# First loads, S5 tables and first norm reordered at the head of a two-block kernel

## The chip, the core and the metric

The kernel runs on one core of a Trainium2 chip. The metric is the device time of one execution in microseconds (us), and lower is better. Its engines are named as in the profile: PE (TensorE matmul) and PEld (its weight loads), DVE (VectorE), ACT (ScalarE), POOL (GpSimd), and SP, which here only issues transfers. ACT and POOL can issue transfers too. A name with q (ACTq) is the queue side of an engine.

## The reference, cut to what matters

Two model blocks run one after the other on 512 tokens of width 1024. The change touches only the head of the first block: the norm, the projection `w_in`, and the preparation of the S5 mixer.

```
h = rmsnorm(x, mix_norm_w)                 # x 512x1024
proj = h @ w_in                            # u 256 | z 768 | xbc 1792 | dt 12 columns
# S5: 16 groups x 64 states
ab = exp(lr*dt) * (cos(li*dt) + i*sin(li*dt))
bu = einsum(u, bb);  h_t = ab * h_(t-1) + bu;  y = Re(einsum(h, c)) + u*d
# SSD: causal conv of 4 taps over xbc, silu; dt = softplus(dt_raw + bias); chunked scan
x = x + concat(y_s5, y_ssd) @ w_out
# then cross attention (mem_n = rmsnorm(mem)), conv-FFN; second block: HGRN2, FoX, routed experts
```

## The kernel before, in words

Activations lie feature by feature: `xt` is 128 partitions x 8 blocks x 512 tokens. Every fp32 operand of a projection is split into a rounded high part (ACT, lines 365 and 489) and the rest (DVE, lines 371 and 495). A projection block of 128 columns is then 8 steps of three matmuls of 128x512 (`pe_fm`, lines 415 to 417): high by high, low by high, high by low. Weights come in slots of 1 MB in a fixed order: `u`, three slots of `x` (called xa), `dt` (half as large), then x and z in turns. SP loads slot g into one of three raw buffers once the DVE has split slot g-3 (`sp_load`, line 357). ACT makes the high part once the matmuls of slot g-2 are done, DVE the low part, PE waits for that.

Each engine runs one instruction list in the order in which the code writes it, with semaphores between the engines. No scheduler is at work. The head of the program, in that order:

- ACT issues seven transfers: the parameters `prm`, `xt` blocks 0 to 3, `row`, `wglu`, the memory `mt`, and two small ones of the router's weights, which only the second block's routing reads. SP issues `xt` blocks 4 to 7, waits for ACT's half, then loads weights.
- S5's angles (`dve_s5_angle`, `act_s5_angle`): a few 128x8 operations, two sines, then nine powers of the rotation by squaring, again on DVE. POOL turns them into tables of cosines and sines over 256 time steps, by doubling: step p makes 2^p new columns for 8 state tiles, six operations of 128 x (8 x 2^p), with p from 0 to 7 (`pool_s5_tables`, lines 749 to 755).
- The first norm: ACT squares (line 450), PE sums them over partitions (line 474), ACT takes ln and exp, then DVE scales a block (line 502), ACT rounds it, DVE takes the rest (line 495), for 8 blocks. PE works on `u`'s first column block as the norm's blocks come, then on its second.
- `dve_s5_matrices` (lines 670 to 707) builds S5's input and output matrices; PE turns them (line 558), DVE copies them (`bt`, line 718).
- Five turns of `x` and `z` blocks follow (`IN_TURNS`). In turn 0 PE runs three x slots, the turn of the matrices, the memory norm's sum, and `dt` with its turn to token order. From turn 1 on each turn also carries a quarter of the S5 scan: PE makes `bu` (line 772), ACT copies it (line 795), and DVE rotates by the tables, scans and rotates back (lines 810 to 849, all 128x1024 but the scans). For an x block ACT empties the bank into `pad` (line 445), applies tap 0 (line 994), DVE the other three taps (line 904), ACT the silu (line 978).

Of the kernel before, what the change touches and what calls it, by code (L numbers as in the profile page):

```python
# [506 lines left out]

# [227 lines left out]

def pool_s5_tables(k):
    G, g, s = k.nc.gpsimd, k.g, k.s
    t1, t2 = k.tt[:, 0, :, :], k.tt[:, 1, :, :]  # L740
    g(G.memset(k.ec[:, :, 0:1], 1.0))
    g(G.memset(k.es[:, :, 0:1], 0.0))
    for p in range(8):
        n = 1 << p
        c, w = (k.pw[:, p, i, :].rearrange("p (j o) -> p j o", o=1).broadcast_to([P, 8, n]) for i in (0, 1))
        lc, ls, hc, hs = k.ec[:, :, 0:n], k.es[:, :, 0:n], k.ec[:, :, n:2 * n], k.es[:, :, n:2 * n]
# [2 lines left out]
        g(G.tensor_tensor(hc, lc, c, ALU.mult))
        g(G.tensor_tensor(t1[:, :, 0:n], ls, w, ALU.mult))  # L750
        g(G.tensor_tensor(hs, ls, c, ALU.mult))
        g(G.tensor_tensor(t2[:, :, 0:n], lc, w, ALU.mult))
        g.own()
        g(G.tensor_tensor(hc, hc, t1[:, :, 0:n], ALU.subtract))
        m = G.tensor_tensor(hs, hs, t2[:, :, 0:n], ALU.add)
        if p == 7:
# [188 lines left out]

def pe_dt(k):
    PE, s = k.nc.tensor, k.s
    pe_fm(k, "dt", 0, 0, k.hi, k.lo, cols=P)
# [4 lines left out]


def act_w_in(k):
    A, s = k.nc.scalar, k.s
# [1 line left out]
    for b in range(4):
        if b == 0:
            A.wait_ge(s.x0, 16)  # L960
        act_square(k, "mix", k.xt, k.sq0, b, T)
    act_s5_angle(k)
    for b in range(4, DB):
        if b == 4:
            A.wait_ge(s.x1, 16)
# [14 lines left out]
    for q, turn in enumerate(IN_TURNS):  # L980
        for x, (part, n) in enumerate(turn):
            stage, slot = in_slot(part, n)
            act_split_to(k, SLOT0[stage] + slot + 1)
            for j in range(2):
# [12 lines left out]
                        silu(blk - 1)  # L997
                else:
                    if n == 0 and j == 0:
                        A.wait_ge(s.s5_tab, 1)  # L1000
                    act_empty(k, i, k.sz[:, 2 * n + j, :], ACT.Silu)
            if part == "x" and n == 6:
                silu(XBC_B - 1)
# [5 lines left out]
                    act_square(k, "mem", k.mt, k.msq, b, MEM)  # L1009
        if q == 0:  # L1010
            act_split_to(k, SLOT0["dt"] + 1)
            act_norm_root(k, "mem", k.rm, k.bank[7][:, 0:MEM], D)
            act_empty(k, BLOCK0["dt"], k.gg[:, 0, 0, :])
            act_ssd_steps(k)


def dve_w_in(k):
    V, s, v = k.nc.vector, k.s, k.v
    dve_s5_angle(k)
    V.memset(k.pad[:, :, 0:3], 0.0).then_inc(s.pads_zero, 1)  # L1020
    dve_split_to(k, 0)
    dve_norm_split(k, "mix", k.xt, k.col("mix_norm", 0, DB), k.sq0, k.rs, k.hi, k.lo, 0, DB, T)
    dve_split_to(k, 1)
    dve_s5_matrices(k)
    for q, turn in enumerate(IN_TURNS):
        step = dve_s5_step(k, q - 1) if q > 0 else iter(())
        for n_, (part, n) in enumerate(turn):
            stage, slot = in_slot(part, n)
            dve_split_to(k, SLOT0[stage] + slot + 1)
            if part == "x":  # L1030
                for j in range(2):
                    blk = 2 * n + j
# [2177 lines left out]
def act_program(k):  # L3210
    A, s, ins = k.nc.scalar, k.s, k.ins
    A.dma_start(k.prm[:, :], ins["params"][0:P * NCOLS].rearrange("(p c) -> p c", p=P)).then_inc(s.params, 16)
    A.dma_start(k.xt[:, 0:4, :], ins["x_t"].rearrange("(k p) c -> p k c", p=P)[:, 0:4, :]).then_inc(s.x0, 16)
    A.dma_start(k.row[:, :], ins["rows"][0:1, :].partition_broadcast(P)).then_inc(s.rows, 16)
    A.dma_start(k.wglu[:, :, :], ins["s5_w_glu"].rearrange("(k p) c -> p k c", p=P)).then_inc(s.wglu, 16)
    A.dma_start(k.mt[:, :, :], ins["mem_t"].rearrange("(k p) c -> p k c", p=P)).then_inc(s.mem, 16)
    A.dma_start(k.wr[:, :, 0:4], ins["w_group_2"].rearrange("(k p) c -> p k c", p=P)).then_inc(s.router, 16)
    A.dma_start(k.wr[:, :, 4:20], ins["w_expert_2"].rearrange("(k p) c -> p k c", p=P)).then_inc(s.router, 16)
# [108 lines left out]
```

## Time and profile before

| what | us |
|---|---|
| median of 3 runs (lowest, highest) | 1674.35 (1672.68, 1676.23) |
| the profiled execution, its own time | 1678.19 |
| its span in the profile | 1676.9 |
| PE busy / DVE busy / ACT busy / POOL busy | 1492.6 / 1042.8 / 756.0 / 136.7 |
| mean granted TensorE clock (of full speed) | 0.939 |

The profiled execution took 1.3 us more than its span, and 3.8 us more than the median. In the page's strip of 40 slices (42 us each) PE is busy for 3 and 8 tenths in the first two slices, 4 tenths around 230 us, 6 around 1320 us and 1 in the last, and 8 or 9 tenths everywhere else. POOL is busy for 5 and 4 tenths in the first two slices and idle for most of the rest.

### The profile page before, as it was taken

What the parts mean: (1) busy time and instruction counts of PE and PEld (TensorE: products, weight loads), DVE (VectorE), ACT (ScalarE), POOL (GpSimd) and SP (SyncE); (2) the same over time, 40 slices, a digit from 0 to 9 for tenths busy, and PEclk for the clock granted to TensorE, in tenths of its full rate; (3) what the DMA queues carried; (4) which work ended last, traced back from release to release, by engine and by line L of the source; (5) the groups of instructions that cost most, each with busy time, mean ns of one, the idle gap of its engine ahead of it and who ended that gap; (6) DMA issues with size and microseconds to landing.
All of it is one profiled execution on the core that took longest, in us unless ns stands there. A gap on an engine that the chain in (4) does not pass through costs nothing.

```text
span 1676.9 us, 17418 instructions
## 1 busy us (share of the span) xinstructions
PE 1492.6 (89%) x6845; PEld 1163.3 (69%) x6845; DVE 1042.8 (62%) x1353; ACT 756.0 (45%) x994; POOL 136.7 (8%) x147
## 2 busy tenths in 40 slices
PE   3889949989988999999999999999988699999981
PEld 1666718857755788788887778786646578888861
DVE  5849976456333455445554648854443588898876
ACT  4453315564432422222223444235345568878763
POOL 5400000000000000000000022300000001111012
PEclk8898969989999999999999999999999799999996
DMA  5121204212210233232222222111002599999974
GB/s 194 63 75 51 75 26 148 74 55 75 76 50 17 106 142 114 75 113 101 101 69 69 102 100 76 51 51 51 26 1 88 215 352 413 410 410 414 407 310 176
DMA packets 41345, 231.57 MB, mean 138 GB/s; under 512 B 6448, under 2 KB 7728, under 8 KB 19120
## 3 DMA queue, kind: packets, MB, share of 16 engines
q1 hardware_dynamic: 29184, 198.75, 31.4%
q0 software_dynamic: 7584, 27.79, 4.4%
q10 hardware_dynamic: 4496, 3.91, 0.8%
q8 instruction: 55, 0.90, 0.2%
q14 instruction: 26, 0.21, 0.0%
HBM read 213.66 MB, written 16.78 MB: 137 GB/s over the span
## 4 chain that ended last, share of the span: by engine, by line
PE 75%; DVE 15%; ACT 5%; issue 3%; DMA 1%; ACTq 1%; POOL 0%; POOLq 0%; DVEq 0%
PE bank L415 14%; PE bank L416 14%; PE bank L417 14%; PE bank L2881 5%; PE bank L2883 5%; PE bank L2882 5%; PE bank L558 3%; DVE w_lo L371 2%; PE bank L434 1%; PE bank L2138 1%; PE bank L2167 1%; DVE bu L837 1%; PE bank L435 1%; PE bank L436 1%; PE bank L474 1%
## 5 line engine op out<-in xcount | busy, mean ns | idle before, releaser
L415 PE MATMUL bank<-h_hi,w_hi 128*128 128x512 f32 x952 | 393.9, 414 | 29.0 <-DVE h_lo L495 16.6
L416 PE MATMUL bank<-h_lo,w_hi 128*128 128x512 f32 x952 | 382.4, 402 | 0.0
L417 PE MATMUL bank<-h_hi,w_lo 128*128 128x512 f32 x952 | 382.0, 401 | 0.0
L371 DVE TENSOR_TENSOR w_lo<-w_raw,w_hi 128x2048 fp32r<-128x2048 f32 (+3 forms) x89 | 197.4, 2218 | 90.8 <-ACT w_hi L365 90.1
L415 PEld LDWEIGHTS bank<-h_hi,w_hi 128*128 128x128 f32 x952 | 183.8, 193 | 88.2 <-DVE h_lo L495 17.8
L417 PEld LDWEIGHTS bank<-h_hi,w_lo 128*128 128x128 f32 x952 | 183.7, 193 | 43.3
L416 PEld LDWEIGHTS bank<-h_lo,w_hi 128*128 128x128 f32 x952 | 184.3, 194 | 41.0 <-issue 1.9
L365 ACT ACTIVATE w_hi<-w_raw 128x2048 fp32r<-128x2048 f32 (+3 forms) x89 | 158.4, 1779 | 60.0 <-PE bank L417 60.0
L3061 DVE TENSOR_TENSOR h_lo<-w_raw,h_hi 128x2048 fp32r<-128x2048 f32 x32 | 73.2, 2291 | 15.4 <-ACT h_hi L2962 15.4
L3061 DVE TENSOR_TENSOR lo_b<-raw_b,hi_b 128x2048 fp32r<-128x2048 f32 x32 | 73.2, 2287 | 8.8 <-ACT hi_b L2962 8.7
L415 PE MATMUL bank<-a_hi,w_hi 128*128 128x512 f32 x176 | 69.4, 394 | 4.5 <-DVE a_lo L1579 4.5
L416 PE MATMUL bank<-a_lo,w_hi 128*128 128x512 f32 x176 | 69.7, 396 | 0.0
L417 PE MATMUL bank<-a_hi,w_lo 128*128 128x512 f32 x176 | 69.2, 393 | 0.0
L1543 ACT ACTIVATE gc<-gc 128x512 f32<-128x512 f32 x22 | 13.9, 632 | 118.6 <-DVE gc L904 118.6
L2962 ACT ACTIVATE hi_b<-raw_b 128x2048 fp32r<-128x2048 f32 x32 | 61.1, 1911 | 6.3 <-PE bank L2883 6.3
L2962 ACT ACTIVATE h_hi<-w_raw 128x2048 fp32r<-128x2048 f32 x32 | 60.9, 1908 | 0.0
L2881 PE MATMUL bank<-h_hi,hh 128*128 128x512 f32 x128 | 53.0, 414 | 5.8 <-DVE hl L3091 4.4
L2881 PE MATMUL bank<-hi_b,xh 128*128 128x512 f32 x128 | 52.9, 413 | 3.1 <-DVE xl L3068 3.1
L1577 DVE TENSOR_TENSOR gc<-gc,bank 128x512 f32<-128x512 f32 x22 | 15.1, 686 | 62.0 <-PE bank L417 62.0
L2882 PE MATMUL bank<-h_hi,hl 128*128 128x512 f32 x128 | 51.5, 403 | 0.0
L2883 PE MATMUL bank<-h_lo,hh 128*128 128x512 f32 x128 | 51.5, 403 | 0.0
L2883 PE MATMUL bank<-lo_b,xh 128*128 128x512 f32 x128 | 51.1, 399 | 0.0
(565 smaller groups left out, 2833.9 us busy)
## 6 DMA issues: line engine op xcount, KB each, us to landing
w_raw<-in_params_dram SPq DMA_DIRECT2D x122, 1024.0 KB, 4.9
raw_b<-in_params_dram SPq DMA_DIRECT2D x51, 1024.0 KB, 8.0
w_raw<-in_params_dram SPq DMA_DIRECT2D x16, 704.0 KB, 4.1
result_rows<-osb POOLq DMA_DIRECT2D x16, 512.0 KB, 8.0
result_rows<-prm POOLq DMA_DIRECT2D x8, 512.0 KB, 3.1
xt<-in_x_t_dram POOLq DMA_DIRECT2D x1, 2048.0 KB, 9.3
scratch_rows<-htm SPq DMA_DIRECT2D x4, 512.0 KB, 3.0
out_dram<-pr SPq DMA_DIRECT2D x4, 512.0 KB, 2.6
```

The costliest lines, as they stand in the source:

```text
L365: A.activation(k.w_hi[:, g % SPLIT, 0:size], k.raw[:, g % RAW, 0:size], ACT.Copy).then_inc(s.w_hi, 1)
L371: V.tensor_tensor(k.w_lo[:, g % SPLIT, 0:size], k.raw[:, g % RAW, 0:size], k.w_hi[:, g % SPLIT, 0:size].bitcast(F32), ALU.subtract).then_i ...
L415: PE.matmul(ps, wh, hi[:, c, 0:width], start=c == 0, stop=False)
L416: PE.matmul(ps, wh, lo[:, c, 0:width], start=False, stop=False)
L417: m = PE.matmul(ps, wl, hi[:, c, 0:width], start=False, stop=c == parts - 1)
L434: PE.matmul(ps, xh, wh, start=c == 0, stop=False)
L558: return k.nc.tensor.transpose(out, in_, k.ident[0:n, 0:n])
L2881: PE.matmul(o, xh[:, k0 + c, :], wh, start=first and c == 0, stop=False)
L2882: PE.matmul(o, xl[:, k0 + c, :], wh, start=False, stop=False)
L2883: m = PE.matmul(o, xh[:, k0 + c, :], wl, start=False, stop=final and c == 3)
L2962: done(A.activation(w_hi[n], raws[n], ACT.Copy), "w", n, c)
L3061: done(V.tensor_tensor(w_lo[n], raws[n], w_hi[n].bitcast(F32), ALU.subtract), "w", n, c)
```

## The change

- **Transfers.** SP's first is now `xt` 0 to 3, then weight slot 0; it waits for `xt` 4 to 7, then loads slots 1 and 2, then `mt`, `row` and `wglu`. ACT issues `prm` and `xt` 4 to 7 only. The router's two go to POOL, behind the zeroing of the result rows.
- **S5.** The two sines come behind the first norm and behind slot 1's high part on ACT; the powers (now `dve_s5_powers`) behind slot 1's low part on DVE; the matrices behind slot 3's low part in turn 0. POOL's tables wait for the powers, and stop at p = 6. DVE makes p = 7, behind the next slot's low part and ahead of the copy of `dt`.
- **PE.** 30 transposes of a constant into a bank that nothing reads come first. `u`'s two blocks take turns at each step of the norm. `dt`'s block comes ahead of the memory norm's sum, and no longer behind the wait for `bt`. Slot 0's low part on DVE lies between the norm's first and second block.

```diff
-def dve_norm_split(k, name, src, gain, sq, rs, hi, lo, off, blocks, width):
+def dve_norm_split(k, name, src, gain, sq, rs, hi, lo, off, blocks, width, slot=None):
...
             dve_norm_lo(k, name, sq, hi, lo, off, b - 1, width)
+        elif slot is not None:
+            dve_split_to(k, slot)
...
+def s5_double(k, engine, step, p):
+    n = 1 << p
...
+    step(engine.tensor_tensor(hc, lc, c, ALU.mult))
+    step(engine.tensor_tensor(t1, ls, w, ALU.mult))
+    step(engine.tensor_tensor(hs, ls, c, ALU.mult))
+    step(engine.tensor_tensor(t2, lc, w, ALU.mult))
+    step.own()
+    step(engine.tensor_tensor(hc, hc, t1, ALU.subtract))
+    return engine.tensor_tensor(hs, hs, t2, ALU.add)
...
+def dve_s5_table(k):
+    V, s = k.nc.vector, k.s
+    V.wait_ge(s.s5_tab, 1)
+    s5_double(k, V, k.v, 7).then_inc(s.s5_tab, 1)
...
 def pe_w_in(k):
+    for _ in range(30):
+        pe_turn(k, k.bank[6][:, 0:P], k.ident[:, :])
     pe_norm_sum_all(k, "mix", k.sq0, T, 7)
-    for j in range(2):
-        pe_fm(k, "u", 0, j, k.hi, k.lo, "mix")
+    for c in range(DB):
+        for j in range(2):
+            pe_fm(k, "u", 0, j, k.hi, k.lo, "mix", first=c, stop=c + 1)
...
             pe_s5_matrices(k)
+            pe_fm(k, "dt", 0, 0, k.hi, k.lo, cols=P)
             PE.wait_ge(s.s5_bt, 4)
             pe_norm_sum_all(k, "mem", k.msq, MEM, 7)
...
 def dve_w_in(k):
     dve_s5_angle(k)
-    dve_split_to(k, 0)
-    dve_norm_split(k, "mix", ..., DB, T)
+    dve_norm_split(k, "mix", ..., DB, T, slot=0)
     dve_split_to(k, 1)
-    dve_s5_matrices(k)
+    dve_s5_powers(k)
...
             dve_split_to(k, SLOT0[stage] + slot + 1)
+            if q == 0 and n_ == 1:
+                dve_s5_matrices(k)
...
             dve_split_to(k, SLOT0["dt"] + 1)
+            dve_s5_table(k)
             V.wait_ge(s.dt_turn, 1)
...
 def sp_program(k):
+    SP.dma_start(k.xt[:, 0:4, :], ...).then_inc(s.x0, 16)
+    sp_load(k, 0)
+    SP.wait_ge(s.x1, 16)
+    for g in range(1, RAW):
+        sp_load(k, g)
+    SP.dma_start(k.mt[:, :, :], ...); SP.dma_start(k.row[:, :], ...); SP.dma_start(k.wglu[:, :, :], ...)
```

ACT's list begins like this before (its seven transfers, then the S5 rate and the squares of the first four blocks of `xt`):

```order
L3212 DMA prm<-in_params_dram 128x774
L3213 DMA xt<-in_x_t_dram 128x4x512
L3214 DMA row<-in_rows_dram 128x52
L3215 DMA wglu<-in_s_w_glu_dram 128x2x256
L3216 DMA mt<-in_mem_t_dram 128x8x256
L3217 DMA w_router<-in_w_group_dram 128x8x4
L3218 DMA w_router<-in_w_expert_dram 128x8x16
L612 ACT_TABLE_LOAD
```

And like this now:

```order
L3249 DMA prm<-in_params_dram 128x774
L3250 DMA xt<-in_x_t_dram 128x4x512
L615 ACT_TABLE_LOAD
L615 ACTIVATE s5sc<-prm 128x8
L617 ACTIVATE s5sc<-s5sc 128x8
L450 ACTIVATE xbc<-xt 128x512 x8
```

Five transfers went off ACT's list, and the sines no longer part the eight squares. On DVE, the end of the angles and the start of the first norm, before:

```order
L647 TENSOR_SCALAR s5sc<-s5sc 128x8
L649 TENSOR_TENSOR s5sc<-s5sc 128x8
L651 TENSOR_SCALAR pw<-s5sc 128x8
L652 COPY pw<-s5sc 128x8
L656 TENSOR_TENSOR s5sc<-pw 128x8
L657 TENSOR_TENSOR s5sc<-pw 128x8
```

Now, at the same place (`pad`'s zeroing, then the norm's first block, slot 0's low part, the norm's second block):

```order
L650 TENSOR_SCALAR s5sc<-s5sc 128x8
L1041 MEMSET pad 128x2x3
L503 SCALAR_TENSOR_TENSOR xbc<-xt,prm,rs 128x512
L371 TENSOR_TENSOR w_lo<-w_raw,w_hi 128x2048
L503 SCALAR_TENSOR_TENSOR xbc<-xt,prm,rs 128x512
L495 TENSOR_TENSOR h_lo<-xbc,h_hi 128x512
```

The powers are gone from in front of the norm, and POOL has nothing to do until they come. On DVE at the end of turn 0, before (the last taps, the copies of S5's matrix, the next slot, the copy of `dt`):

```order
L904 SCALAR_TENSOR_TENSOR xbc<-pad,prm,xbc 128x512 x6
L718 COPY bt<-bank 128x128 x4
L371 TENSOR_TENSOR w_lo<-w_raw,w_hi 128x2048
L1044 COPY dtr<-bank 128x48
L1069 TENSOR_TENSOR sm<-dtr,row 128x48
```

Now:

```order
L727 COPY bt<-bank 128x128 x4
L371 TENSOR_TENSOR w_lo<-w_raw,w_hi 128x2048
L754 TENSOR_TENSOR ec<-ec,pw 128x8x128
L755 TENSOR_TENSOR sz<-es,pw 128x1024
L756 TENSOR_TENSOR es<-es,pw 128x8x128
L757 TENSOR_TENSOR sz<-ec,pw 128x1024
L759 TENSOR_TENSOR ec<-ec,sz 128x8x128
L760 TENSOR_TENSOR es<-es,sz 128x8x128
L1067 COPY dtr<-bank 128x48
```

The last doubling stands in DVE's list ahead of the copy of `dt`.

## Rows read from the trace of the kernel before

**Rows 1.** Chain of waits of the first 260 us: start us, us, what.

```profile
1.40 0.54 ACTq L3213
...
7.63 5.66 ACTq L3218
...
16.00 8.56 PE bank L474 x16
...
28.59 1.60 DVE xbc L502 x2
...
47.46 3.90 DVE w_lo L371
...
66.86 2.30 DVE w_lo L371
...
97.61 5.29 PE bank L474 x16
```

**Rows 2.** Transfers issued in the first 12 us: KB, median us to landing.

```profile
xt<-in_x_t_dram SPq DMA_DIRECT2D x1, 1024.0 KB, 7.4
xt<-in_x_t_dram ACTq DMA_DIRECT2D x1, 1024.0 KB, 8.9
```

**Rows 3.** Timeline of ACT: start us, us, line, operation, count [idle before <- releaser].

```profile
15.24 2.17 ACT L450 ACTIVATE xbc<-xt 128x512 f32<-128x512 f32 x4
```

**Rows 4.** Timeline of PE's weight loads in the first norm's sum.

```profile
16.99 0.34 PEld L474 LDWEIGHTS bank<-xbc,ones 128*128 128x128 f32 x1 [0.52 <-ACT xbc L450]
...
19.24 0.19 PEld L474 LDWEIGHTS bank<-xbc,ones 128*128 128x128 f32 x1 [0.24 <-issue]
```

**Rows 5.** Windows: stretch, length, busy us (count) by engine, PEclk, DMA, GB/s.

```profile
29.00:30.00 1.00, 0.00 (x0) 0.00 (x0) 1.00 (x2) 0.58 (x1) 0.92 (x2) 0.58 0.81 287
31.00:49.00 18.00, 12.99 (x25) 7.03 (x26) 18.00 (x15) 5.58 (x7) 17.61 (x14) 0.50 0.04 16
126.00:157.00 31.00, 29.61 (x113) 20.20 (x113) 28.56 (x32) 10.64 (x15) 0.00 (x0) 0.94 0.20 68
```

**Rows 6.** Timeline of DVE in a later norm, with POOL idle.

```profile
378.91 0.75 DVE L502 SCALAR_TENSOR_TENSOR xbc<-sz,prm,rs 128x512 f32<-128x512 f32 x1
379.57 0.69 DVE L495 TENSOR_TENSOR h_lo<-xbc,h_hi 128x512 fp32r<-128x512 f32 x1
```

**Rows 7.** Timeline of DVE: powers, next work, matrices, a later part of them.

```profile
19.07 0.17 DVE L649 TENSOR_TENSOR s5sc<-s5sc 128x8 f32<-128x8 f32 x1 [2.68 <-ACT s5sc L622]
...
25.07 2.40 DVE L371 TENSOR_TENSOR w_lo<-w_raw,w_hi 128x2048 fp32r<-128x2048 f32 x1
...
51.28 1.85 DVE L670 TENSOR_TENSOR s5sc<-s5sc,pw 128x8 f32<-128x8 f32 x1
...
61.62 0.16 DVE L681 TENSOR_TENSOR s5sc<-s5sc,prm 128x8 f32<-128x8 f32 x1
...
69.07 4.55 DVE L904 SCALAR_TENSOR_TENSOR xbc<-pad,prm,xbc 128x512 f32<-128x512 f32 x6
```

**Rows 8.** Timeline of ACT from the first x slot's last bank on.

```profile
65.85 0.60 ACT L445 ACTIVATE pad<-bank 128x512 f32<-128x512 f32 x1 [3.93 <-PE bank L417]
...
71.42 0.63 ACT L978 ACTIVATE xbc<-xbc 128x512 f32<-128x512 f32 x1 [2.83 <-DVE xbc L904]
...
74.42 1.90 ACT L365 ACTIVATE w_hi<-w_raw 128x2048 fp32r<-128x2048 f32 x1
76.64 0.60 ACT L445 ACTIVATE pad<-bank 128x512 f32<-128x512 f32 x1 [0.32 <-PE bank L417]
...
82.08 0.60 ACT L445 ACTIVATE pad<-bank 128x512 f32<-128x512 f32 x1 [3.46 <-PE bank L417]
```

**Rows 9.** Timeline of DVE at `dt`, of ACT at turn 1's x bank.

```profile
109.76 0.21 DVE L1044 COPY dtr<-bank 128x48 f32<-128x48 f32 x1 [10.01 <-PE bank L558]
...
120.74 0.60 ACT L445 ACTIVATE pad<-bank 128x512 f32<-128x512 f32 x1 [1.49 <-PE bank L417]
```

**Rows 10.** Groups of DVE, 126 to 250 us: count | busy us, mean ns | idle.

```profile
L810 DVE TENSOR_TENSOR gg<-bu,ec 128x1024 f32<-128x1024 f32 x4 | 4.9, 1226 | 12.4 <-ACT bu L795 12.4
```

More of the change, by code:

```diff
@@ L647, in dve_s5_angle, with dve_s5_powers @@
     V.tensor_scalar(th, th, float(np.float32(3.1415925)), float(-np.float32(3.1415925)), ALU.min, ALU.max).then_inc(s.s5_dve, 1)
+def dve_s5_powers(k):
+    V, v, s = k.nc.vector, k.v, k.s
+    mag, cs, sn, abr, abi, fr, fi, lrm, dt, th, q, r, t1, t2, den = s5_scalars(k)
     V.wait_ge(s.s5_act, 4)
@@ L733, in pe_s5_matrices @@
         pe_turn(k, k.bank[4 + n][:, 0:P], bd[:, n // 2, 4 * h:4 * h + 4, :].rearrange("p t c -> p (t c)")).then_inc(s.s5_turn, 1)
+def s5_double(k, engine, step, p):
+    n = 1 << p
+    t1, t2 = k.tt[:, 0, :, 0:n], k.tt[:, 1, :, 0:n]
+    c, w = (k.pw[:, p, i, :].rearrange("p (j o) -> p j o", o=1).broadcast_to([P, 8, n]) for i in (0, 1))
+    lc, ls, hc, hs = k.ec[:, :, 0:n], k.es[:, :, 0:n], k.ec[:, :, n:2 * n], k.es[:, :, n:2 * n]
+    step(engine.tensor_tensor(hc, lc, c, ALU.mult))
[5 more added lines that the diff above has]
+    return engine.tensor_tensor(hs, hs, t2, ALU.add)
 def pool_s5_tables(k):
     G, g, s = k.nc.gpsimd, k.g, k.s
-    t1, t2 = k.tt[:, 0, :, :], k.tt[:, 1, :, :]
     g(G.memset(k.ec[:, :, 0:1], 1.0))
     g(G.memset(k.es[:, :, 0:1], 0.0))
[L743 to L746, printed above, removed]
+    for p in range(7):
         g.own()
         G.wait_ge(s.s5_pow, p + 1)
[L749 to L756, printed above, removed]
+        m = s5_double(k, G, g, p)
+        if p == 6:
             m.then_inc(s.s5_tab, 1)
@@ L805, in dve_s5_step @@
     V.wait_ge(s.s5_buc, 4 * q + 4)
-    V.wait_ge(s.s5_tab, 1)
+    V.wait_ge(s.s5_tab, 2)
+    v.own()
     if q > 0:
@@ L947, in pe_dt @@
     PE, s = k.nc.tensor, k.s
-    pe_fm(k, "dt", 0, 0, k.hi, k.lo, cols=P)
     PE.wait_ge(s.evac_a, EMPTIED[BLOCK0["dt"]][1])
@@ L957, in act_w_in @@
     act_s5_rate(k)
[L958 to L965, printed above, removed]
+    for b in range(DB):
+        if b in (0, 4):
+            A.wait_ge(s.x1 if b else s.x0, 16)
         act_square(k, "mix", k.xt, k.sq0, b, T)
@@ L972, in act_w_in @@
     act_split_to(k, 1)
+    act_s5_angle(k)
     for j in range(2):
@@ L999, in act_w_in @@
                     if n == 0 and j == 0:
-                        A.wait_ge(s.s5_tab, 1)
+                        A.wait_ge(s.s5_tab, 2)
                     act_empty(k, i, k.sz[:, 2 * n + j, :], ACT.Silu)
@@ L1011, in act_w_in @@
             act_split_to(k, SLOT0["dt"] + 1)
+            act_empty(k, BLOCK0["dt"], k.gg[:, 0, 0, :])
             act_norm_root(k, "mem", k.rm, k.bank[7][:, 0:MEM], D)
-            act_empty(k, BLOCK0["dt"], k.gg[:, 0, 0, :])
             act_ssd_steps(k)
@@ L1020, in dve_w_in @@
     V.memset(k.pad[:, :, 0:3], 0.0).then_inc(s.pads_zero, 1)
-    dve_split_to(k, 0)
-    dve_norm_split(k, "mix", k.xt, k.col("mix_norm", 0, DB), k.sq0, k.rs, k.hi, k.lo, 0, DB, T)
+    dve_norm_split(k, "mix", k.xt, k.col("mix_norm", 0, DB), k.sq0, k.rs, k.hi, k.lo, 0, DB, T, slot=0)
     dve_split_to(k, 1)
-    dve_s5_matrices(k)
+    dve_s5_powers(k)
     for q, turn in enumerate(IN_TURNS):
@@ L2327, in pool_zero, with pool_router @@
         G.dma_start(results[n], source).then_inc(s.zeroed, 16)
+def pool_router(k):
+    G, s = k.nc.gpsimd, k.s
+    G.dma_start(k.wr[:, :, 0:4], k.ins["w_group_2"].rearrange("(k p) c -> p k c", p=P)).then_inc(s.router, 16)
+    G.dma_start(k.wr[:, :, 4:20], k.ins["w_expert_2"].rearrange("(k p) c -> p k c", p=P)).then_inc(s.router, 16)
 def pe_w_out2_turn(k, b):
@@ L3189, in sp_program @@
 def sp_program(k):
-    k.nc.sync.dma_start(k.xt[:, 4:8, :], k.ins["x_t"].rearrange("(k p) c -> p k c", p=P)[:, 4:8, :]).then_inc(k.s.x1, 16)
-    k.nc.sync.wait_ge(k.s.x0, 16)
-    for g in range(SLOTS):
+    SP, s, ins = k.nc.sync, k.s, k.ins
+    SP.dma_start(k.xt[:, 0:4, :], ins["x_t"].rearrange("(k p) c -> p k c", p=P)[:, 0:4, :]).then_inc(s.x0, 16)
+    sp_load(k, 0)
+    SP.wait_ge(s.x1, 16)
+    for g in range(1, RAW):
+        sp_load(k, g)
+    SP.dma_start(k.mt[:, :, :], ins["mem_t"].rearrange("(k p) c -> p k c", p=P)).then_inc(s.mem, 16)
+    SP.dma_start(k.row[:, :], ins["rows"][0:1, :].partition_broadcast(P)).then_inc(s.rows, 16)
+    SP.dma_start(k.wglu[:, :, :], ins["s5_w_glu"].rearrange("(k p) c -> p k c", p=P)).then_inc(s.wglu, 16)
+    for g in range(RAW, SLOTS):
         sp_load(k, g)
@@ L3202, in pool_program @@
     pool_zero(k)
+    pool_router(k)
     pool_mix(k)
@@ L3212, in act_program @@
     A.dma_start(k.prm[:, :], ins["params"][0:P * NCOLS].rearrange("(p c) -> p c", p=P)).then_inc(s.params, 16)
[L3213 to L3218, printed above, removed]
+    A.dma_start(k.xt[:, 4:8, :], ins["x_t"].rearrange("(k p) c -> p k c", p=P)[:, 4:8, :]).then_inc(s.x1, 16)
     act_w_in(k)
```

## The prediction

> **What bounds the kernel now.** I read the page's strip first: PE is busy nearly everywhere but in the first slice and around 230 us. The change works on the first 126 us, so I followed the chain of waits there [rows 1], then the timelines of single engines.
>
> The chain begins on ACT. It issues transfers until 7.63 + 5.66 = 13.3 us, the last a small router load. ACT's half of `xt`, issued at 1.40 [rows 1], landed 8.9 later, at 10.3, and SP's half, its first transfer, issued at about 0.9, landed 7.4 later, at 8.3 [rows 2]. The squares start at 15.2 [rows 3]. PE sums from 16.00 to 24.56, and DVE scales the first block at 28.59 [rows 1], so 4.03 us of ACT lie between. The norm's split takes DVE from 28.59 to 47.46, 18.9 us for 16 operations, 1.18 each [rows 1]. A later norm, with POOL idle, goes from one operation to the next in 379.57 - 378.91 = 0.66 us [rows 6]. POOL's table work lies beside the slow one, and the low part of slot 1 takes 3.90 beside it where slot 2's takes 2.30 alone [rows 1]. So the two engines take turns at something. Then DVE builds the matrices from 51.28 to 66.86 [rows 7, 1], PE stands until 69.2, finishes its third x slot at 92.9 (82.08 + 2 x 5.44 [rows 8]), waits for `bt` until 97.61, sums for 5.29, and does `dt` [rows 1]. DVE waits 10.0 us and copies `dt` at 109.76 [rows 9]. From 126 to 250 us DVE sets the pace: busy for 28.56 of 31.0 us [rows 5], and what idle time is left is mostly the 12.4 us for `bu` in four turns [rows 10].
>
> **The change, step by step, in the profiled execution's time.**
>
> *Start.* ACT issues two transfers instead of seven and is free at 2 us (1.40 + 0.54 [rows 1]). SP's first load should land as its first did, at 8.3 us. The squares start there, and PE's sum 0.76 later as before (15.24 to 16.00) [rows 1, 3], at 9.1. It took 8.56. Its weight loads show a slow phase, 0.34 each until nearly 19 us, then 0.19 [rows 4]: 3 us at half rate, of which a warm start saves 1.5. The 30 transposes would give that warm start if the clock is held over the 1 or 2 us between; after PE stopped at 24.56 the fall came within the window 29 to 30 [rows 5], which speaks for it. Bounds: end at 16.1 or 17.7; I take 16.5, nearer to the held clock. DVE scales at 16.5 + 4.0 = 20.5 instead of 28.6: 8.1 gained.
>
> The Trainium skill (DMA: Bandwidth & Descriptors, section Queues, rings and completion order) says that each DMA engine goes round-robin between the queue rows that have work. That speaks against the new order: slot 0 now follows on SP's queue and would take half the engines' time from ACT's `xt` half. No row has this mix. By that rule the half that landed at 10.3 would lose about 2 us more; PE needs its fifth block at 9.1 + 4 x 0.86 = 12.5, so the sum stays as it is, or loses under 1 us.
>
> *Split.* 16 operations at 0.66, plus slot 0's low part, 2.3 (before, it lay in the wait for the norm): 12.9, so DVE ends at 33.4. Slot 1's high part follows the last rounding, and its low part ends at about 37. PE starts `u` after the first low part, at 20.5 + 0.66 + 2.3 + 1.3 = 24.8. Two steps of `u` are 6 matmuls. A block of 24 matmuls takes 5.44 us at the full clock (82.08 - 76.64) [rows 8], 0.227 each; at half clock 6 of them need 2.6 us, more than DVE's 1.3, so PE is never idle and should leave the low clock, as it did in the norm's sum, in 3 us. `u` ends at 24.8 + 10.9 + 1.5 = 37.2, where slot 1 is ready. The first x slot ends at 37.2 + 10.9 = 48.1. Before, that was 65.8 [rows 8].
>
> *To the matrices.* On ACT the way from that slot's last bank to the end of slot 3's high part took from 65.85 to 76.32 with 2.83 of waiting for DVE's taps [rows 8]: 7.6 without. The wait should go, as DVE is ahead: powers 6.0 (25.07 - 19.07 [rows 7]) to 43, slot 2's low part to 45 to 47, taps of the first block (half of 4.55, rows 7; more beside POOL) to 50. So slot 3's high part ends at 55.7, its low part at 58.0. POOL's p = 4 to 6 fall in 44 to 58; I add 1.0 for operations that wait one POOL operation, so 59.0. The other slots on PE end at 48.1 + 2 x 10.9 = 69.9; PE is not the bound.
>
> *DVE to `dt`.* The matrices took 15.6 beside POOL; the part from 61.62 on, alone, took 5.2 [rows 7, 1]. The nine operations before it are of the 0.2 us kind, 1.7 in all: 6.9, to 65.9. Then 12 taps, 2 x 4.55 [rows 7], with `dt`'s low part, half of 2.3, between: 10.3, to 76.2. Four copies of `bt` of 0.2 and a low part: 3.1, to 79.3. The last doubling: 6 x 1.2 [rows 10] = 7.2, to 86.5. PE meanwhile does `dt` from 72 to 77, sums by 82 and turns `dt` by 83: the order that put 5.4 us of `dt` into the wait for `bt` now makes DVE the later one. Without the table DVE would wait for PE instead, so 3.5 of its 7.2 are on the path. The copy of `dt` comes at 86.5 instead of 109.76: 23.3 gained.
>
> *To S5.* Before, ACT waited 1.49 for PE at the last x bank [rows 9]; now PE has that bank at 94, ACT comes at 96, so the 1.5 is gained too. Total 24.8. I take off 0.6 for the extra wait between engines in the ping-pong of taps and silus: 24.2. The scan's turns follow unchanged, as nothing in them has an absolute time. The router's loads cost nothing on POOL: the page's strip shows it idle there, and their first reader is the second block's routing.
>
> 1678.2 - 24.2 = 1654.0 in the profiled execution. The median of the runs lies 3.8 below it, so 1650.2.
>
> **Rivals.**
>
> *A. DVE and POOL share more than I charge.* p = 0 to 6 now lie beside the powers, slot 2 and the taps of the first x slot. From 28.6 to 51.3 DVE did 10.6 + 2.3 of work in 22.8 us, so the pair cost 9.9, and the nine small operations of the matrices lost about 8.6 (51.28 to 61.62 [rows 7] less 1.7). What moved to DVE was under that last loss. If all of the first 9.9 comes back on the path, the gain is 24.2 - 9.9 + 1.0 = 15.3: 1659. For it: DVE is nearly the bound there. Against: DVE has slack until 56 us, where ACT is the later one.
>
> *B. The clock stays low through `u`.* 48 matmuls at 0.43 are 20.5 instead of 12.4: 8 lost, some in DVE's slack, gain 16 to 18: 1657. For it: from 31 to 49 us PE was at 0.50 [rows 5]. Against: it was busy for 13.0 of those 18 us, and now its work is dense.
> The Trainium skill (TensorE: Matmul & The Clock Gate, Part 1) says that the idle state is the throttled one and that activity releases it, so an idle stretch behind the 30 transposes can undo them. By that rule the sum would end at 17.7, and 1.2 us of the gain go; the trace agrees that it falls after idling, but only 4.5 us later.
>
> *C. More than I think:* DVE's and ACT's exchange of taps and silus closes up, slot 3 comes earlier, PE is the bound to 70 and DVE copies at 83: gain 28, 1646.
>
> *D. Slower: the scan's turns become PE's.* In 126 to 250 us PE has 113 matmul records a turn beside DVE's 31 us, at a clock of 0.94 in the first [rows 5]. If its clock fell in the turns, since it is ahead and waits more, it would need 113 x 0.227 = 25.7 us at full and 51 at half clock. From a quarter of its matmuls at half clock on PE decides instead of DVE; the 24 are lost when each of some 3.3 turns costs 7.3 more, that is when half of them run so, and at all of them it is slower by 3.3 x 20 - 24 = 42: 1676 to 1716. Against: before, PE idled by the same pattern and fell only to about 0.9.
>
> *E. Nothing gained:* a hidden wait, as for a load behind `mt`, holds turn 0 at its old time: 1674. Slots 1 and 2 have over 15 us to land, which speaks against it.
>
> **How the numbers follow.** Forecast 0.66, its own range 1646.5 to 1655. A 0.14, B 0.08, C 0.08, D 0.02, E 0.02. The range 1645 to 1660 holds the forecast and nearly all of A, B and C. The bound for same is 0.2%, 3.3 us, about what a measurement of this kernel can tell. Faster 0.96, same 0.02, slower 0.02.
>
> **What would show it.** Right: the first norm sum starting near 9 and DVE scaling at 20 to 22; 0.66 from one norm operation to the next; PE without a gap from 25 to 70; DVE without a gap from 59 to 87; POOL ending its tables before 60; the turns of 31 us as before. Wrong: a sum that starts after 11 (the transfers), norm operations over 0.9 (not POOL, then), a gap ahead of x slot 2 or 3 on PE, a copy of `dt` after 92, or turns longer than 32.

## The result and the profile after

The changed kernel takes 1653.2 us (median of 4 runs, 1651.9 to 1654.5), the kernel before, on the same chip, 1673.5 us. The ratio is 0.9879, 95% interval 0.9864 to 0.9894: 20.3 us faster, 3 us less than forecast, inside the range. The profiled execution took 1652.19 us (span 1651.0).

The chain of waits of the kernel after, from its first 90 us (start us, us, what), answers [rows 1]:

```profile
1.40 11.18 DMA xt<-in_x_t_dram
12.60 0.64 ACT xbc L450
13.28 3.71 PE bank L474 x8
...
21.02 0.75 DVE xbc L503
21.78 2.20 DVE w_lo L371
...
55.76 1.82 ACT w_hi L365
57.60 3.02 DVE w_lo L371
...
79.92 2.20 DVE w_lo L371
82.12 1.14 DVE ec L754
```

ACT's seven transfers no longer lead the chain: `xt` does. From 57.6 to 89 us it lies on DVE without a break. The transfers of the kernel after (issuing queue, KB, median us to landing) answer [rows 2]:

```profile
xt<-in_x_t_dram SPq DMA_DIRECT2D x1, 1024.0 KB, 7.4
xt<-in_x_t_dram ACTq DMA_DIRECT2D x1, 1024.0 KB, 11.2
```

SP's half lands as before, ACT's takes 11.2 instead of 8.9 us and lands at 12.6. The timelines of ACT and of PE (start us, us, what, [idle before <- releaser]) show the squares and the norm's sum in two parts, with that hole between them [rows 3]:

```profile
8.31 2.19 ACT L450 ACTIVATE xbc<-xt 128x512 f32<-128x512 f32 x4 [1.72 <-DMA xt<-in_x_t_dram]
12.60 2.19 ACT L450 ACTIVATE xbc<-xt 128x512 f32<-128x512 f32 x4 [2.10 <-DMA xt<-in_x_t_dram]
```

```profile
8.99 3.70 PE L474 MATMUL bank<-xbc,ones 128*128 128x512 f32 x8 [1.02 <-ACT xbc L450]
13.28 3.70 PE L474 MATMUL bank<-xbc,ones 128*128 128x512 f32 x8 [0.59 <-ACT xbc L450]
```

Both parts take 3.70 for 8 matmuls, the full clock's pace; the slow first 3 us of [rows 4] are gone. The timeline of DVE of the kernel after, in the norm, at the first small operations of the matrices, and from `bt` to the first rotation, answers [rows 7, 9]:

```profile
25.16 0.74 DVE L503 SCALAR_TENSOR_TENSOR xbc<-xt,prm,rs 128x512 f32<-128x512 f32 x1
25.82 0.68 DVE L495 TENSOR_TENSOR h_lo<-xbc,h_hi 128x512 fp32r<-128x512 f32 x1
...
57.60 3.02 DVE L371 TENSOR_TENSOR w_lo<-w_raw,w_hi 128x2048 fp32r<-128x2048 f32 x1 [3.05 <-ACT w_hi L365]
60.54 1.24 DVE L679 TENSOR_TENSOR s5sc<-s5sc,pw 128x8 f32<-128x8 f32 x1
61.70 0.15 DVE L680 TENSOR_TENSOR s5sc<-s5sc 128x8 f32<-128x8 f32 x1
61.78 1.26 DVE L681 TENSOR_TENSOR s5sc<-s5sc 128x8 f32<-128x8 f32 x1
...
79.05 0.88 DVE L727 COPY bt<-bank 128x128 f32<-128x128 f32 x4
...
88.98 0.20 DVE L1067 COPY dtr<-bank 128x48 f32<-128x48 f32 x1
...
104.09 1.23 DVE L832 TENSOR_TENSOR gg<-bu,ec 128x1024 f32<-128x1024 f32 x1 [1.94 <-ACT bu L816]
```

Norm operations follow each other at 0.66 us, as where POOL is idle [rows 6]. The low part of slot 3 takes 3.02 instead of 2.3, and two small operations last 1.25, because POOL's tables end only at 63.0 (timeline of POOL, kernel after):

```profile
58.54 3.21 POOL L759 TENSOR_TENSOR ec<-ec,sz 128x512 f32<-128x512 f32 x1
61.72 1.30 POOL L760 TENSOR_TENSOR es<-es,sz 128x512 f32<-128x512 f32 x1
```

The windows of the kernel after (stretch, length, busy us (count) of PE, PEld, DVE, ACT, POOL, then PEclk, DMA, GB/s) answer [rows 5]; the third and fourth go from one turn's first rotation to the next:

```profile
25.00:28.00 3.00, 2.61 (x6) 2.17 (x7) 3.00 (x6) 1.57 (x3) 0.00 (x0) 0.50 0.82 322
31.00:49.00 18.00, 18.00 (x81) 14.89 (x80) 15.00 (x52) 9.07 (x11) 10.76 (x30) 1.00 0.25 78
104.09:135.67 31.58, 31.35 (x114) 21.76 (x113) 28.56 (x33) 10.94 (x15) 0.00 (x0) 0.88 0.20 67
135.67:168.12 32.45, 31.80 (x114) 21.80 (x113) 28.56 (x33) 10.93 (x15) 0.00 (x0) 0.87 0.18 65
```

From 31 to 49 us PE works at 2.4 GHz without a gap (granted 1.00), where it stood for 5 of the 18 us and worked at 1.2 GHz (0.50). In the first turn DVE's busy time is the same 28.56 us, but PE is busy for nearly the whole turn at a mean clock of 0.88. That is no mark of the changed kernel: cut from rotation to rotation, the kernel before has one turn at 0.94 and one at 0.87 (windows, kernel before):

```profile
126.24:157.54 31.30, 29.91 (x114) 20.50 (x113) 28.56 (x33) 10.95 (x15) 0.00 (x0) 0.94 0.19 68
157.54:189.40 31.86, 31.49 (x114) 21.72 (x113) 28.55 (x33) 10.94 (x15) 0.00 (x0) 0.87 0.19 66
```

The group of the first rotations, 104 to 228 us after (count | busy us, mean ns | idle), answers [rows 10]; DVE waits 13.5 instead of 12.4 us there:

```profile
L832 DVE TENSOR_TENSOR gg<-bu,ec 128x1024 f32<-128x1024 f32 x4 | 4.9, 1226 | 13.5 <-ACT bu L816 13.5
```

**Where the time came from.** In the profiled executions, the copy of `dt` comes 20.8 us earlier (109.76 to 88.98), the first rotation 22.15 (126.24 to 104.09), and the first rotation of the fourth turn 21.3 (224.75 to 203.47). After that both kernels run the same code. The same norm operation is 23.0 earlier (378.91 [rows 6] to 355.94), the same low part further on 25.5 (timelines of DVE, before, then after):

```profile
621.36 2.29 DVE L371 TENSOR_TENSOR w_lo<-w_raw,w_hi 128x2048 fp32r<-128x2048 f32 x1 [1.11 <-ACT w_hi L365]
```

```profile
595.83 2.29 DVE L371 TENSOR_TENSOR w_lo<-w_raw,w_hi 128x2048 fp32r<-128x2048 f32 x1 [1.11 <-ACT w_hi L365]
```

Those last 4 us are not the change's. From the first rotation of the fourth turn to this low part the code is the same in all fourteen traces of this document, and that stretch took from 391.3 to 396.6 us in them; before it was 396.6, the longest, after it was 392.4. The profiled execution of before also lay 4.7 above its median (1678.2 to 1673.5), that of after 1.0 below its own. What the change gave by the end of the stage, 21.3, is about the 20.3 of the medians.

### The profile page after: what moved, and what is told of

Read it like the earlier page. It is cut to its first block, busy times and chain, and to the rows that moved or that the text cites. A ratio compares the mean times of both kernels' runs of the same rounds, so it can differ in the third digit from the quotient of the medians.

```text
span 1651.0 us, 17477 instructions
## 1 busy us (share of the span) xinstructions
PE 1485.6 (90%) x6875; PEld 1163.2 (70%) x6875; DVE 1034.1 (63%) x1359; ACT 756.0 (46%) x994; POOL 121.3 (7%) x143
## 4 chain that ended last, share of the span: by engine, by line
PE 75%; DVE 13%; ACT 6%; issue 4%; DMA 2%; POOL 0%; POOLq 0%; ACTq 0%; DVEq 0%
PE bank L415 14%; PE bank L416 14%; PE bank L417 14%; PE bank L2910 5%; PE bank L2912 5%; PE bank L2911 5%; PE bank L561 3%; DVE w_lo L371 2%; PE bank L434 1%; PE bank L2161 1%; PE bank L2190 1%; PE bank L435 1%; PE bank L436 1%; DVE xbc L926 1%; DVE bu L859 1%
## 5 line engine op out<-in xcount | busy, mean ns | idle before, releaser
L1566 ACT ACTIVATE gc<-gc 128x512 f32<-128x512 f32 x22 | 13.9, 632 | 118.5 <-DVE gc L926 118.5
```

## The experiments

Three marks are read in every trace, in us from its start: DVE's copy of `dt`, the first S5 rotation (called the marker in the expectations), and the first rotation of the fourth turn. The marks come from one profiled execution each. Where the ratio says "one execution", the time does too; otherwise times are medians, and each ratio is to the kernel before on the same chip (its medians lay from 1673.3 to 1674.7).

| kernel | time us | ratio [95%] | copy of `dt` | first rotation | fourth turn |
|---|---|---|---|---|---|
| before | 1673.5 | 1 | 109.76 | 126.24 | 224.75 |
| after | 1653.2 | 0.9879 [0.9864, 0.9894] | 88.98 | 104.09 | 203.47 |
| after, again | 1653.0 | 0.9868 [0.9845, 0.9891] | 88.87 | 105.28 | 203.31 |
| loads only | 1666.9 | 0.9962 [0.9948, 0.9975] | 103.17 | 119.28 | 217.72 |
| powers first | 1657.4 | 0.9905 [0.9888, 0.9922] | 92.74 | 109.16 | 207.38 |
| last table on POOL | 1663.8 | 0.9944 [0.9923, 0.9964] | 97.03 | 113.16 | 212.22 |
| no transposes | 1656.0 | one execution | 90.72 | 106.78 | 203.41 |
| sum first | 1654.2 | one execution | 92.73 | 109.05 | 206.58 |
| slot 0 later | 1651.4 | one execution | 88.79 | 104.48 | 203.32 |
| `u` in a row | 1655.0 | one execution | 89.37 | 105.79 | 202.44 |
| split early | 1648.9 | 0.9853 [0.9836, 0.9870] | 86.68 | 103.05 | 199.80 |
| early, squares late | 1652.0 | 0.9863 [0.9846, 0.9879] | 89.29 | 105.70 | 203.71 |
| squares late | 1656.7 | 0.9888 [0.9862, 0.9914] | 91.01 | 107.14 | 203.80 |
| early, matrices late | 1651.3 | 0.9872 [0.9855, 0.9889] | 86.71 | 101.84 | 201.23 |

**1. Loads only.** The kernel before, with the new `sp_program`, `act_program` and `pool_router` and nothing else.

> The kernel before with the new order of loads alone (SP, ACT and GpSimd). Marker in all runs: the start of the first S5 rotation on DVE, at 126.2 us before and 104.1 after the change. Theory (terms add): the first norm sum ends near 17 to 17.7 instead of 24.6, DVE scales at 21 to 22, everything behind it shifts by 7 to 8: marker near 118.5, time 0.4 to 0.5% less than before. Rival (the transfers gain only beside the rest, as DVE works on S5's powers when the norm comes): marker above 122. The second half of xt lands near 12.6 by either.

The theory came near: the first rotation came 7.0 us earlier, the medians differ by 7.8 and the ratio says 6.4. The sum's start moved from 16.00 to 9.23, but the sum took 9.25 instead of 8.56 (PE timeline), and the norm's operations on DVE stayed at 1.1 to 1.75 us beside POOL. So the order of the loads is about a third of the change's gain; the rest needs the other edits.

**2. Powers first.** The changed kernel with the S5 powers (and the sines) back ahead of the norm, so that POOL works beside it:

```
 def dve_w_in(k):
     dve_s5_angle(k)
+    dve_s5_powers(k)
...
     dve_split_to(k, 1)
-    dve_s5_powers(k)
```

> The changed kernel with sines and powers back in front of the first norm, so that POOL's doublings 5 and 6 lie beside the norm. Theory (POOL and DVE hold each other up): norm operations go from 0.66 to 1.0 to 1.4 us apart while POOL works, the last low part ends near 40 to 43 instead of 33.6, but POOL is done before the matrices, which saves 3: marker near 107 to 109 instead of 104.1. Rival (slow norm operations come from something else, as the clock or the transfers): the norm stays at 0.66 apart and the marker falls below 103.

Timeline of DVE in the norm of "powers first":

```profile
32.92 1.52 DVE L495 TENSOR_TENSOR h_lo<-xbc,h_hi 128x512 fp32r<-128x512 f32 x1
37.49 1.77 DVE L503 SCALAR_TENSOR_TENSOR xbc<-xt,prm,rs 128x512 f32<-128x512 f32 x1
39.19 0.68 DVE L495 TENSOR_TENSOR h_lo<-xbc,h_hi 128x512 fp32r<-128x512 f32 x1
```

The operations are long until POOL ends its tables at 38.7 us and 0.68 at once after it. The norm's split ended 8.3 us later, yet the copy of `dt` only 3.8: DVE's matrices now ran alone. So moving POOL's work away from the norm, as the change does, only put off 4.5 of those 8.3 us and won 3.8.

**3. Last table on POOL.** The changed kernel with `for p in range(8)` in the tables again and no `dve_s5_table`.

> The changed kernel with the last doubling (p = 7) back on POOL. Theory: POOL works on it from 63 to about 80 us beside the matrices and the taps, each small DVE operation waits up to 2.3 us for POOL, which costs DVE 9 to 12, more than the 7.1 of the doubling on DVE: the copy of dt at 91 to 94 instead of 89.0, marker 106 to 109. Rival (POOL's work is free there): the copy of dt at 85 to 86 as PE's turn of dt allows, marker near 101.

POOL ended at 75.5, and DVE's small operations waited for each of its six in turn. Timelines, POOL first, then DVE:

```profile
65.14 1.90 POOL L755 TENSOR_TENSOR sz<-es,pw 128x1024 f32<-128x1024 f32 x1
66.99 1.90 POOL L756 TENSOR_TENSOR es<-es,pw 128x1024 f32<-128x1024 f32 x1
```

```profile
67.09 1.82 DVE L689 TENSOR_TENSOR s5sc<-s5sc 128x8 f32<-128x8 f32 x1
68.84 0.15 DVE L690 TENSOR_TENSOR s5sc<-s5sc,prm 128x8 f32<-128x8 f32 x1
69.03 1.75 DVE L692 TENSOR_TENSOR s5sc<-s5sc 128x8 f32<-128x8 f32 x1
```

An operation of 0.15 us lasts until POOL's current one is over (L756 ends at 68.9), the next slips through, the third waits again. The matrices' first zeroing came at 75.79 instead of 65.01. That is 10.8 us for six POOL operations, and some 7 us of DVE work buys it off. The copy of `dt` came at 97.03, where I had 91 to 94: it is 8.1 later, 10.8 less the 7 that DVE saves and plus 4.1 in which DVE now waits for PE, which the late matrices had held up.

**4. No transposes.** The 30 transposes ahead of the sum left out.

> The changed kernel without the 30 transposes. Theory (they warm PE for the norm's sum, which has only 0.6 us to gain since the second half of xt lands late): the sum starts at half clock, its first eight pieces take 5 instead of 3.7, it ends at 17.2 to 17.6 instead of 17.0, marker +0.3 to +0.7. Rival (the clock rises late as the sum pauses for the second half): all 16 pieces slow, sum ends after 19, marker +2 or more.

```profile
9.11 9.70 PE L474 MATMUL bank<-xbc,ones 128*128 128x512 f32 x16 [9.11 <-ACT xbc L450]
```

PE's timeline, above: 9.70 in one piece, with slow weight loads (0.34) until 13.9, against 3.70 + 3.70 around a hole of 0.6. The sum ended 1.84 later, the copy of `dt` 1.7, the rotation 2.7. That is the rival's size, though not its mechanism: the loads were slow only for the first 4.8 us. But at the first rotation of the fourth turn the kernels were level again (203.41 to 203.47 us), since here the first two turns lasted 30.65 us each instead of 31.58 and 32.45. Experiment 9 shows that these lengths vary between executions, so what the transposes are worth in the kernel's time is open.

**5. Sum first.** `pe_fm(k, "dt", ...)` behind the memory norm's sum again, ACT in the same order.

> The changed kernel with the memory norm's sum ahead of dt's block on PE, as before. Theory: PE waits for bt until 79.9, sums until 84 to 85, does dt until 90 and its turn until 91: the copy of dt at 91.5 to 92 instead of 89.0, marker +2.5 to +3. Rival (DVE's doubling still covers it): marker +0.

```profile
92.73 0.21 DVE L1067 COPY dtr<-bank 128x48 f32<-128x48 f32 x1 [3.29 <-PE bank L561]
```

DVE, which has no wait here in the kernel after, waits 3.29 for PE: the copy is 3.75 later (0.4 of it stood already at the copies of `bt`, as `xt` landed late in this execution). The reordered `dt` block is worth about what my sum of DVE and PE said, 2.5 to 3.

**6. Slot 0 later.** SP loads slot 0 behind its wait for ACT's half of `xt`.

> The changed kernel with weight slot 0 issued only after the second half of xt has landed. Theory (slot 0 on SP's queue takes a share of the DMA engines from ACT's half): that half lands at 10.3 instead of 12.6 us and the sum on PE ends near 16; but slot 0 lands at 18 to 19, and ACT's list has its high part ahead of the logarithm, so DVE scales at 23.5 to 25 instead of 21.0: marker +2.5 to +4. Rival (the half is late for another reason, as the order behind prm): it still lands near 12.6.

Transfers and PE's sum:

```profile
xt<-in_x_t_dram ACTq DMA_DIRECT2D x1, 1024.0 KB, 8.7
```

```profile
9.06 7.13 PE L474 MATMUL bank<-xbc,ones 128*128 128x512 f32 x16 [1.46 <-ACT xbc L450]
```

Without slot 0 beside it ACT's half takes 8.7 again and the hole in the sum closes; slot 0's high part comes late (15.11) and holds the root up, and nothing is left of it at the copy of `dt` (0.2). So slot 0 did cost the second half 2.5 us, and it did not matter. The rest of the theory missed: it had slot 0 land at 18 to 19 us and DVE scale at 23.5 or later, and DVE scaled at 20.99.

**7. `u` in a row.** `u`'s two blocks one after the other as before.

> The changed kernel with u's two blocks one after the other. Theory: the first block goes at the norm's pace (3 matmuls per 1.27 us, all of it at half clock) and ends near 35, the second takes 5.5 at full or 10 at half clock: u ends at 40.5 to 45 instead of 38.3, marker +2 to +7. Rival (turns are worth nothing, as DVE is the bound to the matrices): marker within 0.5.

The end of `u` came 1.1 us later, the copy of `dt` 0.4, and the marker 1.7, which is under the 2 to 7 of the theory and about what it varies by itself (experiment 9). PE ran at the low clock only until 30.6 here too. The turns of `u` are a small part of the change, at most.

**8. Split early.** The changed kernel with slot 0's low part ahead of the norm's first block, into the wait for the root:

```
-    dve_norm_split(k, "mix", ..., 0, DB, T, slot=0)
+    dve_split_to(k, 0)
+    dve_norm_split(k, "mix", ..., 0, DB, T)
```

> The changed kernel with slot 0's low part on DVE ahead of the norm, in the wait for it. Its high part is done at 16.6 and DVE idles from 7.6 to 21.0, so theory: the first low part of the norm and PE's first matmul come 2.2 earlier, PE is the bound from there to the end of the first x slot, marker -2.2 (101.9). Rival (the path runs over ACT or DVE further on): marker -1 or less.

```profile
16.65 2.29 DVE L371 TENSOR_TENSOR w_lo<-w_raw,w_hi 128x2048 fp32r<-128x2048 f32 x1 [8.97 <-ACT w_hi L365]
21.05 1.42 DVE L503 SCALAR_TENSOR_TENSOR xbc<-xt,prm,rs 128x512 f32<-128x512 f32 x2 [2.11 <-ACT rs L483]
```

The low part lies in idle time and ends before the root is there. All of its 2.3 us reach the copy of `dt` (86.68). The marker gained only 1.0, which was the rival's size; the next experiment shows how little the marker says about 1 us.

**9. The changed kernel again**, to see what belongs to an execution.

> The changed kernel once more, as the measure for the two beside it. Theory (what differs between executions of one kernel is where the stretches of low granted clock fall in the turns): first S5 rotation again within 0.3 us of 104.1 us, each turn 30.7 us long or up to 32.5 us, and the time within 2 us of 1653. Rival (the lengths of the turns belong to the kernel): spacings of 31.6, 32.5 and 35.4 us again.

The copy of `dt` was the same to 0.1 us, the rotation 1.2 later: both theories missed that. PE's timelines, first the kernel after, then the repeat, then "split early":

```profile
100.94 2.48 PE L793 MATMUL bank<-u,bt 32*128 32x512 f32 x4 [2.15 <-ACT bu L816]
```

```profile
100.83 3.78 PE L793 MATMUL bank<-u,bt 32*128 32x512 f32 x4 [3.78 <-ACT bu L816]
```

```profile
98.65 3.74 PE L793 MATMUL bank<-u,bt 32*128 32x512 f32 x4 [1.04 <-ACT bu L816]
```

In the repeat PE ran `dt`'s block at a granted clock of 1.00, where the kernel after had 0.56 to 0.65 from 74.7 to 79 us. So it came 1.7 us sooner to the matmuls of the scan and idled 3.78 instead of 2.15 us for ACT. The granted clock then fell at about 100.5, ahead of these four matmuls; in the kernel after it fell at about 102.3, in the middle of them. At full clock the same four take 1.98. "Split early" shows that the idle time just ahead does not decide it: after 1.04 us they took 3.74. From the copy of `dt` to the rotation it is 15.1 to 16.5 us in all kernels of the table, whatever they change. The first rotation is thus good to 1.4 us only, and the copy of `dt`, which came again to 0.1 in the one repeat, is the better mark. The turns were 31.1, 31.6 and 35.3 us: the third is 35.3 in every trace and belongs to the kernel, the first two vary with the execution; "split early" had 30.70 twice (windows from rotation to rotation):

```profile
103.05:133.75 30.70, 29.65 (x114) 20.69 (x113) 28.55 (x33) 10.94 (x15) 0.00 (x0) 0.94 0.19 69
133.75:164.45 30.70, 29.56 (x114) 20.70 (x113) 28.56 (x32) 10.94 (x15) 0.00 (x0) 0.94 0.19 68
```

Over all fourteen traces a first or second turn with a mean clock of 0.94 or 0.95 lasted 30.6 to 31.3 us, one with 0.87 or 0.88 31.6 to 32.45, with the same work on DVE. The two together lasted 61.3 to 64.0, so a mark behind them is good to some 3 us only.

**10. Squares late**, alone and with the early split. The memory norm's squares on ACT from step 0 of turn 0 to step 1 (`if x == 1 and q == 0`), to free slot 3's high part.

> The changed kernel with only the memory norm's eight squares on ACT moved behind the blocks of slot 3. Theory (DVE's row of work is the bound and waits 2.5 us for slot 3's high part, most of it for these squares): the first S5 rotation at about 102 instead of 104.1 us, time 1651 us. Rival (DVE reaches the low part later here than with the early split, so little of that wait is there to win): rotation 103.5 to 104.1 us and no change of the time.

> The changed kernel with two moves: slot 0's low part ahead of the first norm's first block on DVE (as in the run with the early split), and the memory norm's eight squares on ACT one step later in turn 0, behind the blocks of slot 3 instead of ahead of slot 3's high part. Theory (DVE's row of work sets the start of the S5 stage, and its 3.04 us wait for slot 3's high part at 54.85 us is part of it): that part starts at 50.5 instead of 52.9 us, DVE's low part at about 52.4 instead of 54.85, the copy of dt at 84.3 instead of 86.68 and the first S5 rotation at about 100.7 us instead of 103.05; time about 1646.5 us, 6 below the changed kernel. Rival (the sum of the memory norm or a weight behind it ends last, and the later squares push that): the rotation stays at 103 us or comes later, time 1648 to 1650 us.

Both theories fell, and so did the rival of "squares late", which saw no loss; the rival of the pair, a marker at 103 or later, fits. The copy of `dt` came 2.0 us later, and with the early split 2.6 us later than in experiment 8 (0.7 of that from a later landing of `xt`). Timeline of ACT, "squares late":

```profile
71.21 0.63 ACT L999 ACTIVATE xbc<-xbc 128x512 f32<-128x512 f32 x1 [8.35 <-DVE xbc L926]
71.74 2.54 ACT L450 ACTIVATE msq<-mt 128x256 f32<-128x256 f32 x8
74.19 1.04 ACT L365 ACTIVATE w_hi<-w_raw 128x1024 fp32r<-128x1024 f32 x1
```

The squares now stand behind a silu that waits for DVE's taps until 71.2, and in front of the next slot's high part, which DVE waits for. ACT's 8.35 us of idle time lie ahead of that silu, not behind it. And the gain at slot 3 did not come either: DVE had its low part 1.05 us earlier, yet the zeroing of the matrices stood at 64.89, as in the repeat (64.90). POOL ended at 63.5 in both; until it is done, an earlier DVE only waits more.

**11. Early split, matrices late.** The matrices past POOL's tables, behind `dt`'s low part (`if q == 0 and n_ == 2`).

> The early-split kernel (slot 0's low part ahead of the first norm's first block) with S5's matrices moved on DVE from behind slot 3's low part to behind the low part of dt's slot, so past the taps of one slot and past the end of POOL's tables. Theory (their small operations are long only beside a POOL operation, and what was lost there is had back once POOL is done at 60 us): DVE runs the six taps at 57.7 to about 64.5 us, the matrices at about 65.5 to 70.8 us (5.2 instead of 9.0 us), the copy of dt comes at about 85.1 instead of 86.68 us, PE no longer waits 3.04 us for dt's low part, the first S5 rotation at about 101.5 instead of 103.05 us; time about 1647.5 us. Rival (the taps beside POOL grow by as much as the small operations shrink, or PE, which is ready for the matrices at 68.8 us, waits for them and passes that on): copy of dt and first rotation where they were or later, time 1649 us or more.

Timeline of DVE:

```profile
57.87 7.16 DVE L926 SCALAR_TENSOR_TENSOR xbc<-pad,prm,xbc 128x512 f32<-128x512 f32 x6
...
66.08 0.16 DVE L679 TENSOR_TENSOR s5sc<-s5sc,pw 128x8 f32<-128x8 f32 x1
...
76.78 0.87 DVE L727 COPY bt<-bank 128x128 f32<-128x128 f32 x4
```

The matrices shrank as expected (66.08 to 72.3, no 128x8 operation over 0.2), but the six taps that took their place beside POOL took 7.16 instead of 4.56, and `bt` was copied at 76.78 against 76.75. This is the rival, by the copy of `dt`: what POOL costs DVE is paid by whatever stands there. The marker came 1.2 earlier, within what it varies by. The time, 1651.3, is not told apart from either kernel.

The fastest median is the early split's, 1648.9. That it beats the kernel before, by 24 us, is shown. That it beats the changed kernel too is likely, not shown: the copy of `dt` says 2.3 us and the medians 4, but the two intervals overlap.

## Why the prediction was right, point by point

- *The start* held. Squares at 8.31 (8.3 forecast), DVE scaling at 21.02 (20.5). Of the 0.5, the hole in the sum (0.6) is the cause: the prediction put the loss from the second transfer at under 1 us, and the sum ended at 16.98 instead of 16.5. The Trainium skill (DMA: Bandwidth & Descriptors, section Queues, rings and completion order) says that engines go round between the queues with work; the trace agrees, 8.9 became 11.2 us with slot 0 beside it and 8.7 without.
- *The warm start* held: 7.4 us of matmuls instead of 8.56. It was worth 1.8 us at the end of the sum (experiment 4), 1.5 had been put down. Rival B's form of it (the idle stretch behind the transposes undoes them) did not come: PE stood for 1.0 us, and both parts ran at the full clock's pace.
- *The norm's split* held: 0.66 a step, slot 1's low part ending at 37.0. Rival A had 8.9 us come back later. What came back is 0.7 at slot 3's low part (3.02 for 2.3) and 2.2 in the matrices (8.4 for 6.2), against the 1.0 that was charged: some 2.
- *`u`* was sized too small: 1.5 us were put down for the slow clock at its start. The 3 us of slowness came from [rows 4]; here the granted clock stayed at 0.50 for the first 5.2 us, twelve matmuls of 0.43 instead of 0.23, so 2.4 were lost. PE also started 0.6 late. It reached slot 1 at 38.8 instead of 37.2, the first x slot's end at 49.9 instead of 48.1.
- *POOL's end* is the term that was mis-sized most. I had p = 4 to 6 in 44 to 58 us and all of it before 60; it ended at 63.0. So the matrices took 8.4 instead of 6.9. Even the 6.9 was off, by luck in the helpful direction: before L681 stand eight small operations and not nine, and experiment 11 has them in 0.98 us instead of 1.7, the matrices alone in 6.2. POOL's price there was thus 2.2. Slot 3's low part ended at 60.6 instead of 59.0 (0.6 from the start, 1.0 from `u`), the matrices at 69.0 instead of 65.9, and the rest took 0.6 less than computed: the copy of `dt` at 88.98 instead of 86.5. Experiments 3 and 11 show that it is POOL: with more of its work beside them the matrices grow by 10.8, past its end they shrink to 6.2.
- *DVE as the later one at `dt`* held. DVE had no gap from 57.6 to 89, PE waited 2.42 us for `dt`'s low part. PE had turned `dt` by 86.0, 3.0 ahead of DVE (3.5 forecast), and putting the sum first again cost 3.7 at the copy.
- *The 0.9 at the last x bank* can't be confirmed: it was 1.4 in one execution of the changed kernel and 0.1 in the other.
- *"The turns follow unchanged"* is not contradicted. The three turns took 98.5 us before, 99.4 after and 98.0 in the repeat. What rival D describes is in the trace, PE busy for 31.35 of 31.58 us at a clock of 0.88, but it is in the kernel before as well (31.49 of 31.86 at 0.87), and it is far from the price that would have made the kernel slower.
- Two of the prediction's own signs went against it: POOL ended its tables at 63.0, not before 60, and the second turn was 32.45, where over 32 was to mean wrong. The first is the mis-sized term above. The second was set too tightly: the repeat had 31.56, and "loads only" had 32.44 as well.
- The total is 3.0 us short of the forecast, and 2.5 of it stand at the copy of `dt` (20.8 gained, 23.3 forecast). The 22.15 at the first rotation look better by luck of the execution: the repeat had 21.0. The 24.2 was taken from a profiled execution 4.7 above the median of its runs; at the end of the stage it was 21.3.

## What to carry to other kernels

Ask of every move beside a second engine on a shared resource who takes its place there: moving POOL's work away from the norm, or DVE's small operations away from POOL, gave back half or more of what it took (4.5 of 8.3 us, 2.6 of 2.8), while doing the work on DVE itself brought the copy of `dt` 8 us forward. Of an operation that is moved into "idle time", look at which side of the waiting instruction the idle time lies. Judge a change in one stage by a mark that the bounding engine sets alone; marks behind a PE that waits move with its clock, by up to 1.4 us here and by some 3 after two more turns.

## What the runs showed of the hardware

- DVE and POOL take turns by whole operations. DVE work of 0.15 us on 128x8 elements lasted 1.25 us beside POOL's 128x512 and 1.7 to 2.2 beside its 128x1024 (experiment 3), six taps 7.16 instead of 4.56 (experiment 11). POOL pays too: its 128x512 operation of 1.03 us lasted 3.21 beside DVE's 128x2048 low part (kernel after, at 58.54). The Trainium skill (SBUF — State Buffer, section SBUF: two separate sides) calls the pair of ports that they share an exclusive lock, not a split of bandwidth; the rows of experiment 3 agree.
- The same four matmuls of 32x512, at the same place of the program, took 1.98 us at a granted clock of 1.00 and 3.78 at 0.50. The idle time ahead of them does not tell which: 2.48 us after 2.15 idle and 3.78 after 3.78 in two executions of one kernel, but 3.74 after 1.04 in "split early".
- Started idle, PE ran slow for 4.8 us of the sum in experiment 4 (slow loads from 9.1 to 13.9), where the kernel before had 3 us. The clock column reads 1.00 in both stretches, so this slowness is seen in the durations alone.
